# The block sums of the condition modulation move from VectorE's reductions to halving adds on GpSimd

## What is computed

```
def second_block(x, c, w_ada, b_ada, ...):
    mod = einsum('bd,dm->bm', silu(c), w_ada[l]) + b_ada[l]        # 6 * 1024 numbers
    shift1, scale1, gate1, shift2, scale2, gate2 = split(mod[:, None, :], 6, axis=-1)
    h = rms_norm(x, g_norm1[l]) * (1 + scale1) + shift1
    ...
```

## Time and profile before

| what | value |
| --- | --- |
| median of 3 runs (lowest to highest) | 1331.9 us (1331.81 to 1333.97) |
| span of the profiled execution | 1331.0 us |
| TensorE busy | 1305.0 us, 98% |
| VectorE busy | 995.2 us, 75% |
| ScalarE busy | 652.6 us, 49% |
| GpSimd busy | 102.8 us, 8% |
| last feed-forward steps and the modulation | 331 to 366 us of the span |

### The profile page before, as it was taken

The page is one execution under the profiler, slowest core; times in us unless marked ns, Lnnn a source line. Parts: engine busy times, 40 slices in busy tenths (PEclk is TensorE's granted clock), DMA queues, the critical chain, the costliest instruction groups (busy, mean ns, idle before and its releaser), DMA issues.

```text
span 1331.0 us, 17698 instructions
## 1 busy us (share of the span) xinstructions
PE 1305.0 (98%) x7304; PEld 1106.1 (83%) x7304; DVE 995.2 (75%) x1258; ACT 652.6 (49%) x623; POOL 102.8 (8%) x136
## 2 busy tenths in 40 slices
PE   8999899999899999999999999999999999999998
PEld 5878788888688887988888888888888888888887
DVE  6557778888876876589989899998475666666664
ACT  6554564444356455455565455555554444444441
POOL 1101200000020000000000001010110000000000
PEclk9999999999999999999999999999999999999999
DMA  9515279997352225557776678988998888888860
GB/s 365 204 54 190 104 293 355 384 371 297 132 205 101 91 73 197 171 181 237 236 247 222 222 238 269 285 260 266 325 359 298 288 286 294 296 292 293 290 230 32
DMA packets 113358, 317.26 MB, mean 238 GB/s; under 512 B 7168, under 2 KB 73984, under 8 KB 91648
## 3 DMA queue, kind: packets, MB, share of 16 engines
q1 hardware_dynamic: 95232, 249.03, 52.7%
q0 software_dynamic: 18048, 67.12, 14.4%
HBM read 281.51 MB, written 34.60 MB: 237 GB/s over the span
## 4 chain that ended last, share of the span: by engine, by line
PE 89%; DVE 6%; ACT 2%; issue 1%; DMA 1%; POOL 0%; SPq 0%; DVEq 0%; ACTq 0%
PE psum L504 87%; DVE slab_lo L1648 2%; PE psum L507 2%; DMA slab_raw<-in_w_in 1%; DVE arena L1926 1%; DVE arena L1924 1%; ACT arena L1331 0%; ACT slab_hi L1222 0%; ACT arena L1245 0%; DVE arena L2066 0%; ACT arena L1368 0%; POOL statistics L456 0%; DVE residual L2372 0%; DVE arena L2370 0%; ACT arena L1259 0%
## 5 line engine op out<-in xcount | busy, mean ns | idle before, releaser
L1648 DVE TENSOR_TENSOR slab_lo<-slab_raw,slab_hi 128x2048 fp32r<-128x2048 f32 x206 | 469.6, 2287 | 174.5 <-ACT slab_hi L1222 174.4
L1222 ACT ACTIVATE slab_hi<-slab_raw 128x2048 fp32r<-128x2048 f32 x206 | 392.6, 1911 | 228.8 <-PE psum L504 227.9
L504 PE MATMUL psum<-slab_hi,x_parts 128*128 128x512 f32 x1520 | 482.0, 392 | 3.6 <-ACT x_parts L1254 1.8
L504 PE MATMUL psum<-x_parts,slab_hi 128*128 128x512 f32 (+1 forms) x1344 | 420.1, 370 | 1.5 <-ACT arena L1453 0.9
L504 PEld LDWEIGHTS psum<-slab_hi,x_parts 128*128 128x128 f32 x1520 | 285.3, 188 | 67.0 <-ACT x_parts L1254 4.5
L504 PE MATMUL psum<-x_parts,slab_lo 128*128 128x256 f32 x1184 | 331.5, 280 | 0.0
L504 PE MATMUL psum<-slab_lo,x_parts 128*128 128x512 f32 x760 | 295.9, 389 | 0.0
L504 PEld LDWEIGHTS psum<-x_parts,slab_hi 128*128 128x128 f32 x1344 | 241.7, 188 | 46.3 <-ACT arena L1453 1.2
L504 PEld LDWEIGHTS psum<-x_parts,slab_lo 128*128 128x128 f32 x1184 | 223.9, 189 | 0.0
L504 PEld LDWEIGHTS psum<-slab_lo,x_parts 128*128 128x128 f32 x760 | 142.8, 188 | 29.0 <-issue 0.5
L504 PE MATMUL psum<-slab_hi,weighted_hi 128*128 128x512 f32 x296 | 116.6, 394 | 0.7 <-DVE weighted_lo L1945 0.7
(11 more groups left out here) (269 smaller groups left out, 1076.0 us busy)
## 6 DMA issues: line engine op xcount, KB each, us to landing
slab_raw<-in_ex_u SPq DMA_DIRECT2D x128, 512.0 KB, 5.4
slab_raw<-in_ex_v SPq DMA_DIRECT2D x64, 1024.0 KB, 6.5
arena<-in_w_ada SPq DMA_DIRECT2D x24, 1024.0 KB, 7.2
slab_raw<-in_w_gu SPq DMA_DIRECT2D x22, 1024.0 KB, 7.3
slab_raw<-in_w_in SPq DMA_DIRECT2D x21, 1024.0 KB, 5.8
hidden_store<-arena POOLq DMA_DIRECT2D x32, 512.0 KB, 6.5
gates_store<-arena POOLq DMA_DIRECT2D x8, 2048.0 KB, 12.1
arena<-hidden_store POOLq DMA_DIRECT2D x32, 512.0 KB, 5.4
```

What stands on the lines that cost most here:

```text
L504: return PE.matmul(out, lhsT, rhs, start=start, stop=stop)
L1222: ACTE.activation(slab_hi[:, slot, :], raw[:, slot, :], ACT.Copy).then_inc(hi_made[slot], 1)
L1648: DVE.tensor_tensor(slab_lo[:, slot, :], raw[:, slot, :], slab_hi[:, slot, :].bitcast(f32), ALU.subtract).then_inc(lo_made[slot], 1)
```

## The change

GpSimd sums the blocks. Each third needs five adds in place (16, 8, 4, 2 and 1 columns of each of 64 blocks), the last into `ada_rows`, and each add waits for the one before it. That makes 15 adds and 15 signals of `ada_folded`. VectorE makes the three transposes together in step 9, then builds `fold`, and has no modulation work in step 10. The third transpose goes to `ada[:, 1, :]`, so it waits for the second, which reads that place. `ada_rows` and `fold` move to the place of `ada[:, 0, :]`. TensorE's spread waits for `fold_made` and for `ada_folded` at 15.

```
 IN_ORDER = {
-    "pool_filled": (("half_set", 1), ("ada_cleared", 3), ("ml_rows_cleared", 1)),
+    "pool_filled": (("half_set", 1), ("ada_cleared", 3), ("ada_folded", 15), ("ml_rows_cleared", 1)),
...
+    "ada_blocks": (("ada_turned", 3), ("fold_made", 1)),
...
-        ada_rows, fold = carve(10240, 6 * D // 32), carve(10240 + 6 * D // 32, 7 * 32)
+        ada_turned = [ada_raw[:, 0, :], ada_raw[:, 1, :], ada[:, 1, :]]
+        ada_rows, fold = carve(0, 6 * D // 32), carve(6 * D // 32, 7 * 32)
...
                     POOL.wait_ge(*after("block2_constants_loaded", 80))
                     POOL.tensor_copy(sb_mask_b, c2["sb_mask"])
                     POOL.tensor_copy(ml_mask_b, c2["ml_mask"]).then_inc(sem("masks_cast"), 1)
+                    for n3 in range(3):
+                        blocks = ada_turned[n3].rearrange("p (b j) -> p b j", j=32)
+                        POOL.wait_ge(*after("ada_turned", n3 + 1))
+                        for step, half in enumerate((16, 8, 4, 2, 1)):
+                            if step:
+                                POOL.wait_ge(*after("ada_folded", 5 * n3 + step))
+                            to = blocks[:, :, 0:half] if half > 1 else ada_rows[:, 64 * n3:64 * n3 + 64].unsqueeze(2)
+                            POOL.tensor_tensor(to, blocks[:, :, 0:half], blocks[:, :, half:2 * half], ALU.add).then_inc(
+                                sem("ada_folded"), 1)
                 POOL.wait_ge(*after("variance_made", k + 1))
...
-            PE.wait_ge(*after("ada_reduced", 1))
+            PE.wait_ge(*after("fold_made", 1))
+            PE.wait_ge(*after("ada_folded", 15))
...
-            def sum_blocks(n):
-
-                turned = ada_raw[:, n % 2, :]
+            def turn_blocks(n):
                 DVE.wait_ge(*after(f"ada_summed{n}", KT))
-                V.after()
-                V(DVE.transpose(turned, ada[:, n, :]))
-                V.after()
-                return DVE.tensor_reduce(ada_rows[:, 64 * n:64 * n + 64], turned.rearrange("p (b j) -> p b j", j=32), AX.X, ALU.add)
+                DVE.transpose(ada_turned[n], ada[:, n, :]).then_inc(sem("ada_turned"), 1)
...
                 if c == KT + 1:
+                    turn_blocks(0)
+                    turn_blocks(1)
+                    DVE.wait_ge(*after("ada_turned", 2))
+                    turn_blocks(2)
+                    DVE.wait_ge(*after("ada_turned", 1))
                     V(DVE.memset(fold, 0.0))
                     V.after()
-                    V(DVE.tensor_reduce(fold[:, 96:P], ident[:].rearrange("p (g i) -> p i g", g=4), AX.X, ALU.add))
-                    for n in range(2):
-                        V(sum_blocks(n))
-                if c == KT + 2:
-                    sum_blocks(2).then_inc(sem("ada_reduced"), 1)
+                    DVE.tensor_reduce(fold[:, 96:P], ident[:].rearrange("p (g i) -> p i g", g=4), AX.X, ALU.add).then_inc(
+                        sem("fold_made"), 1)
```

## The result

The changed kernel takes 1352.7 us (median of 4 runs, 1349.9 to 1354.5) against 1332.9 us (1331.8 to 1336.0) for the kernel before in the same comparison. The ratio is 1.014, with a 95% interval of 1.0127 to 1.0152: 17 to 20 us slower. A second set of runs of the same kernel gave 1352.7 us again, and a ratio of 1.0138 (1.0124 to 1.0153).

What follows compares the result with a forecast made beforehand. TensorE's products were taken to bound the kernel, with the spread waiting for GpSimd's adds behind the constants. Spread delay 16.2 us plus clock 1.0 us gave +17.2 us on 1331.9: 1349.1 us, range 1341 to 1356.

Steps and rivals of the forecast that it cites:

- What bounds, and where the change acts: TensorE's products hold 87% of the chain; the change matters only at the spread, where GpSimd's list decides.
- VectorE's part: VectorE in steps 9 and 10: low parts start 2.5 us earlier, hidden rows come at 345.0 instead of 347.53.
- When GpSimd may begin: GpSimd's list: adds stand behind mask copies that wait for the constants' DMA; copies from 354.9, first add at 355.4.
- What fifteen adds cost: GpSimd's adds: 5952 elements at 2.15 ns plus 15 times 0.25 us, 16.5 us; bounds 6.7 to 20.8.
- The sum: Spread starts at 372.0 instead of 355.79, +16.2 us; with the clock, +17.2 us in total.
- clock term: TensorE's 18 products behind the spread run at lowered clock after idling 20 us: +1.0 us, bounded by 0 and 3.3.
- The rival on the other side: GpSimd is not held by the constants: spread at 351.9, time 1328, or no change with two meetings; chance 4%.
- four low parts: In that rival, the VectorE instructions beside which the adds would run, each meeting perhaps costing 2.0 us.
- two meetings: In that rival, adds collide twice with VectorE's low parts, putting the spread at 355.9: no change, chance 1%.
- That nothing is won back: Everything behind the spread waits for it, so nothing runs ahead in the gap and none of the loss is recovered later.

Runs made afterwards that it cites:

- VectorE-only run: Changed kernel without GpSimd's adds: VectorE makes three transposes in step 9 and three reductions at the end of step 10; 1333.4 us, 1.0001 to the kernel before.
- two runs that free them in different ways: Changed kernel with adds ahead of the mask copies, 1337.25 us, or with constants loaded before the feed-forward loop, 1336.1 us; ratios to the kernel before 1.0029 and 1.0020.

## Why the prediction was right

**What bounds, and where the change acts.** Right. The one place is the spread, and GpSimd's list decides it. The page of the changed kernel has GpSimd's adds (`POOL arena L464`) in the chain that ended last with 1% of the span, in the place of the reductions.

**VectorE's part.** Hidden rows 12.6 us after the mark were forecast (345.0 less 332.37), 12.4 measured. The regrouping alone is worth nothing, as the VectorE-only run shows.

**When GpSimd may begin.** Mask copies were forecast at 354.9, 22.5 us after the mark; they came at 22.4. That the constants held the adds is shown by two runs that free them in different ways and agree to 0.1 us.

**What fifteen adds cost.** Forecast 2.15 ns for each element and 0.25 us fixed, 16.5 us. Measured 2.15 ns, 0.16 + 0.07 us, and 15.95 us. That the price per element came out to the digit is luck: it came from adding one more read to a copy, and the row behind it was a single shape of 128 elements. The Trainium skill's figure for an add of 2048 float32 elements (GPSIMD Engine Reference, section 3.1, Elementwise — side-by-side cycle accounting), 4497 ns, agrees: the line through the five shapes, carried on to 2048, gives an estimate of 0.16 + 2048 x 2.15 ns = 4.56 us.

**The sum.** The spread was forecast at 39.6 us after the mark (372.0 less 332.37), and came at 39.0 and 39.3. The clock term of 1.0 us stands against 0.4 and 1.3 us. The forecast was 1349.1 us, the median 1352.7, inside the range of 1341 to 1356. By the ratio the loss is 17 to 20 us, by the first profile 17.5, by the forecast 17.2. That the last two agree so well is partly chance: 1.0 us of the 17.5 lay ahead of the mark, and the stage itself cost 15.6 + 0.4 us. Of the 3.6 us between forecast and median, 1.0 us is the base, since the kernel before has a median of 1332.9 in this comparison and not 1331.9. What else the medians have beyond the first profile was not traced, but for the store in the second one.

**The rival on the other side.** Its mechanism was right and its time was not. I wrote that with GpSimd's list free the time would fall to 1328, or show no change with two meetings. The two runs that freed the list were 3 to 5 us and 1 to 4 us slower than the kernel before. What failed is the number of meetings. Their price, 2.0 us each from one pair of powers, held: the three adds that met a low part took 2.0 to 2.2 us more each. But I wrote "four low parts" and counted two meetings, where VectorE makes three low parts while the adds run and each of them met an add. Three at 2.0 us would have put the spread at 357.9, which is 25.5 us after the mark; it came at 25.3. I also left out the other side: the low part of slab 54 grew by 1.4 us, and TensorE's products wait for it. With all fifteen adds ahead this is hidden by the adds, which end later still. So the place behind the constants is not the only thing wrong with the change: three thirds on GpSimd lose to three reductions of 2.29 us even when nothing else holds them.

**That nothing is won back.** Right: in the first profile the distance from the spread to the end is 976.1 us and was 975.2. The clock takes 0.4 us of the difference, and another 0.4 us arise behind 757 us, in the expert stage.

## What to carry to other kernels

Moving work to an idle engine pays by that engine's queue, not by its idle time: before the move, find the wait at which its list stands when the work becomes ready, and who waits for the result. Move only as much as the idle engine finishes beside work that does not share its access to memory; here five of fifteen adds, four of them beside transposes and the last where nobody waited for it, gained 1 to 3.5 us, and fifteen behind the constants lost 17 to 20. And free only what comes last: the 2.7 us by which VectorE's hidden rows came earlier were worth nothing as long as the modulation ended later than they did.

## What the hardware showed that I had not expected

- An add on GpSimd with both inputs in SBUF and a subtraction on VectorE with both inputs in SBUF delay each other in both directions: a 64-element add took 2.30 us instead of 0.30, one of 512 elements 3.20 instead of 1.26, and a subtraction of 2048 elements 3.69 instead of 2.28. Each meeting cost the add 2.0 to 2.2 us, and there were three of them whether ten or fifteen adds ran beside the three low parts. Beside 128x2048 block transposes of VectorE the transposes did not grow (three take 6.85 us with adds beside them, 6.84 without) and the adds grew by about 5% at most. The Trainium skill (SBUF — State Buffer, Who interferes with whom) states that a VectorE instruction with two inputs in SBUF contends with a GpSimd one that reads SBUF; these rows agree with it.
- The half-speed stretch of TensorE does not sit where the kernel puts it. In the kernel before it lay behind the spread, for about 3.4 us. With one useless matmul, and the same list up to its last wait, it lay ahead of the spread, from about 349.3 to 352.7, where the wait for the reduction hid it. With two thirds on GpSimd it fell at 350.7 into products that were waited for. In the changed kernel it reached 4.4 us behind the spread in one execution and 6.4 us in another, and this moved a stretch of ten us by 0.9 us. So a difference of one or two us in one profile behind a wait says little, and the timed runs have to decide.
